# An mLSTM cell whose k-v product is taken as three fp32r products, from parts of v and k that GpSimd splits

## The chip, the cores and the metric

The kernel runs on one NeuronCore of a Trainium2 chip. The metric is the device time of one execution in microseconds (us); the figure compared is the median over runs. Each profile shown is of one execution, whose own time stands beside its span.

## What is computed

The reference is one inference step of a two-layer streaming encoder, for a prompt of 512 tokens and a sample of 64. Layer 1 holds an mLSTM with 4 heads of width 512. The change touches only the state update of the prompt in that cell. Cut to that, the reference reads:

```
dlog = b[t] - b[s] + i[s], masked causal;  m_t = max(inter, max dlog);  w = exp(dlog - m_t)
num  = s_inter * (q C) + ((q k^T) * w) v          # numerator of h
den  = s_inter * (q n) + sum((q k^T) * w)
h    = num / max(|den|, exp(-m_t))
kw   = k * w_s                                     # k weighted by its row of the last token
C_new = dec * C + kw^T v                           # the k-v product: 512 x 512 out of 512 tokens
```

The prompt starts from C = 0, so for it C_new is the product kw^T v alone, written out as the state of 512 x 512 of each head. All of it is in float32.

## The kernel before

Everything stays in one program with one instruction stream for each engine, synchronised by semaphores. Weights come as 1 MB slabs: SyncE loads a slab into `raw` (two buffers), GpSimd splits it into an fp32r high part `whi` and a low part `wlo` (`split`, lines 494 and 501: four pieces of 512 columns, for each a tensor_scalar for the high part and a tensor_tensor subtraction for the low one), and TensorE takes every projection as three fp32r products: high by high, low by high, high by low (`project`, line 596). `split` of slab n waits for `slab_begun` to reach n, that is, for TensorE to have begun slab n-1.

PSUM is used in groups of four banks, alternately even and odd (`group_open`, `group_close`, `group_ready`): a group can be opened only when the group two before it in the order of `schedule()` has been freed by whoever evacuated it.

The mLSTM cell handles the heads in the order 3, 2, 1, 0; the text calls them turn 0, 1, 2 and 3 (n in the code). In each turn TensorE runs, in this order, the groups `smp` (the sample's small products and transposes), `kT` (transposes of k), `den`, `num` (numerator; stationary is v in token order, `mvt`), `kv` (the k-v product), `kvs` (the sample's), `mean`, then the next head's `score`, `var`, and the next head's `vT` (transposes of v). All of these in float32 through the helper `mm` (line 630). `kv` is 16 products a head: for each of 4 output banks d and 4 token blocks j, stationary `mkt[:, j, 128 d ..]`, moving `mvt[:, j, :]` of 512 columns. In turn 2 the four slabs of `ml_out` for the first pair of heads are put in front of `num`, `kv`, `kvs` and `mean`.

Around it:

- VectorE, in turn n from 1 on: `cell_out(n-1)` (lines 2584, 2585 and 2593: twelve instructions that make the output of the head before), then four instructions of line 2625 (k by its weights, for the sum n), which ScalarE adds up (lines 1679, 1680); then the causal mask of the next head (2552), the reciprocal, the scaling of `sz`, the evacuation of `num`, three sums, the evacuation of `kvs` (2659), the subtraction of the mean (2666).
- ScalarE: the copies of v into `mvt` (1578, `turned`), the two high parts of `high_y` (1646), the copies of k into `mkt` (1666), the sums, the issue of the loads of the next head's q, k and v (1685 to 1687), and only then the absolute values of `den` (1690 to 1692), which free the `den` group. `kv` uses the same half of PSUM as `den` and so waits for that.
- GpSimd has no work of the cell's: it has split the slab `ml_out, 1, 0` and waits for turn 2.

```
                act.wait_ge(S("cell_qs"), n + 1)
                load(mq[:], A["t_q"][nxt], "cell_q")
                load(mk[:], A["t_k"][nxt], "cell_k")
                load(mv[:], A["t_v"][nxt], "cell_v")
            g = GR["cell", h, "den"]
            group_ready(act, g)
            act.activation(tm[:, 1, 0:TP], bank(g, 0), ACT.Abs)
```

Of the kernel before, what the change touches and what calls it, by code (L numbers as in the profile page):

```python
# [18 lines left out]
F32 = mybir.dt.float32  # L19
F32R = mybir.dt.float32r  # L20
ALU = mybir.AluOpType
# [3 lines left out]
P = 128  # L25
# [3 lines left out]
T = TP + TS  # L29
HALF = T // 2  # L30
NTB = TP // P
# [4 lines left out]
ML_H, ML_T = 4, 4  # L36
ML_DH = ML_T * P
LATE_Z = (3, "z", 1)
CELL_ORDER = (3, 2, 1, 0)
ATT_ORDER = (0, 2, 1)  # L40
OUT_BEFORE = ("num", "kv", "kvs", "mean")
CELL_STEPS = ("smp", "kT", "den", "num", "kv", "kvs", "mean")
MEM = 256
XH = 4
# [36 lines left out]
MEM_SLABS = [(l, *m) for l in range(2) for m in MEM_ORDER]  # L81
# [111 lines left out]
X_LOADED = (16, 32, 32, 32, 32, 32, 32, 32)  # L193
# [35 lines left out]
def program(nc, A):  # L229
    ctx = ExitStack()  # L230
    with ctx:
        def sb(name, shape, dt=F32, on=ctx):
            return on.enter_context(nc.sbuf_tensor(name, shape, dt))
# [3 lines left out]
        def S(name):  # L237
            if name not in sems:
                sems[name] = ctx.enter_context(nc.semaphore(name))
            return sems[name]  # L240
# [3 lines left out]
        x = xt[:, 0:DT * T].rearrange("p (a t) -> p a t", a=DT)  # L244
        x_in = xt[:, 0:DT * (T + 1)].rearrange("p (a t) -> p a t", a=DT)
        xnh = sb("xnh", [P, DT, T], F32R)
        xnl = sb("xnl", [P, DT, T], F32R)
# [24 lines left out]
        def group_ready(eng, g, turn=None):  # L272
            v = g // 2 + 1
            eng.wait_ge(done[g % 2], v if turn is None else turn + v)
# [108 lines left out]
        cst = sb("conv_out", [P, 2, 16, 3], on=ml)  # L383
        mq = sb("mq", [P, ML_T, T], on=ml)
        mk = sb("mk", [P, ML_T, T], on=ml)
        mv = sb("mv", [P, ML_T, T], on=ml)
        xc = sb("xc", [P, ML_T, T], on=ml)
        mla = ExitStack()
# [6 lines left out]
        gcol = gw[:, 0:48 * 32].rearrange("p (n c) -> p n c", c=32)  # L395
        mla.close()
        mlb = ExitStack()
        rrow = sb("rrow", [4, SCW + TS], on=mlb)
        acol = sb("acol", [P, 20], on=mlb)
        causal = sb("causal", [P, P], on=mlb)  # L400
# [6 lines left out]
        mvt = sb("mvt", [P, NTB, ML_DH], on=mlb)  # L407
# [10 lines left out]
        mlr.close()  # L418
        wt = sb("wt", [P, SCW], on=mlb)
        wts = sb("wts", [TS, TS], on=mlb)  # L420
        mkt = sb("mkt", [P, NTB, ML_DH], on=mlb)
        vt5 = sb("vt5", [TS, ML_DH], on=mlb)
        kt5 = sb("kt5", [TS, ML_DH], on=mlb)
        C0 = sb("C0", [P, ML_T, ML_DH], on=mlb)
        qs = sb("qs", [P, ML_T, TS], on=mlb)
        mlb.close()
        ml.close()

        GR, SL = GROUPS, SLABS
# [51 lines left out]
        def _(pool):  # L481
# [44 lines left out]
            mem0 = SL[("mem",) + MEM_SLABS[0]]  # L526
# [5 lines left out]
            c = slice(0, SLAB // 4)  # L532
# [4 lines left out]
            for kk in range(DT):  # L537
                c = slice(SLAB // 8 * kk, SLAB // 8 * (kk + 1))
# [11 lines left out]
                split(j, mem0 // 2, freed_by=GR["rs", "g", j], parts=2)  # L550
            for j in range(2, len(MEM_SLABS) + 2):
                split(j % 2, mem0 // 2 + j // 2, high=False, act_high=4 * (j - 1) + 3, parts=2)
            third = SL["ml_out", 0, 2]
            with pool.Fori(mem0 // 2 + len(MEM_SLABS) // 2 + 1, third // 2) as i:
                split(0, i)
                split(1, i)
            for j in range(2):
                if j == third % 2:
                    split_by_half(j, third // 2)
                else:  # L560
                    split(j, third // 2)
# [12 lines left out]
        def _(pe):  # L574
# [54 lines left out]
            def mm(out, lhsT, rhs, first=True, last=True):  # L629
                return pe.matmul(out, lhsT, rhs, start=first, stop=last)  # L630
# [60 lines left out]
            for part in ("u", "q", "k", "v", "g"):  # L691
                for i in range(2):
                    g, n = GR["rs", part, i], SL["rs", part, i]
# [392 lines left out]
            for n, h in enumerate(CELL_ORDER):  # L1086
                def open_(x):
                    if h == 1 and x in OUT_BEFORE:
                        out_slab(1, OUT_BEFORE.index(x))
                    g = GR["cell", h, x]  # L1090
                    group_open(pe, g)
                    return g, [bank(g, b) for b in range(4)]

                g, B = open_("smp")
                for d in range(ML_T):
                    mm(B[0][0:TS, 0:TS], mk[:, d, TP:T], mq[:, d, TP:T], d == 0, d == ML_T - 1)
                for b, src in ((1, mv), (2, mk)):
                    for d in range(ML_T):
                        ins = pe.transpose(B[b][0:TS, P * d:P * d + P], src[:, d, TP:T], ident[:])
                group_close(ins, g)  # L1100
                g, B = open_("kT")
                for j in range(NTB):
                    for d in range(ML_T):
                        ins = pe.transpose(B[j][:, P * d:P * d + P], mk[:, d, P * j:P * j + P], ident[:])  # L1104
                group_close(ins, g)
                g, B = open_("den")
                pe.wait_ge(S("cell_pt"), n + 1)
                pe.wait_ge(S("cell_qs"), n + 1)
                pe.wait_ge(S("cell_smp"), n + 1)
                pe.wait_ge(S("cell_c"), 16 * (n + 1))  # L1110
                for d in range(ML_T):
                    mm(B[2][0:TS, :], qs[:, d, :], C0[:, d, :], d == 0, False)
                mm(B[2][0:TS, :], wts[:], vt5[:], False, True).then_inc(S("bank_filled"), 1)
                for j in range(NTB):
                    mm(B[0][:, P * j:TP], ones[:], wt[:, blk(j):blk(j) + TP - P * j], j == 0, j == NTB - 1)
                for d in range(ML_T):
                    mm(B[1][:, 0:TS], n0b[:, d, :], qs[:, d, :], d == 0, False)
                mm(B[1][:, 0:TS], ones[0:TS, :], wts[:], False, True)
                pe.wait_ge(S("bank_read"), n + 1)
                for e in range(ML_T):  # L1120
                    ins = pe.transpose(B[3][:, TS * e:TS * e + TS], tm[0:TS, 1, P * e:P * e + P], ident[0:TS, 0:TS])
                group_close(ins, g)
                g, B = open_("num")
                pe.wait_ge(S("cell_vt"), n + 1)
                for e in range(ML_T):
                    for j in range(NTB):
                        ins = mm(B[e][:, P * j:TP], mvt[:, j, P * e:P * e + P], wt[:, blk(j):blk(j) + TP - P * j],
                                 j == 0, j == NTB - 1)
                group_close(ins, g)
                pe.wait_ge(S("cell_kt"), n + 1)  # L1130
                g, B = open_("kv")
                for d in range(ML_T):
                    for j in range(NTB):
                        ins = mm(B[d], mkt[:, j, P * d:P * d + P], mvt[:, j, :], j == 0, j == NTB - 1)
                        if n + 1 == ML_H and (d, j) == (0, 0):
                            ins.then_inc(S("slab_begun"), 1)
                group_close(ins, g)
                g, B = open_("kvs")
                for d in range(ML_T):
                    ins = mm(B[d], kt5[:, P * d:P * d + P], vt5[:])  # L1140
                    if d + 1 < ML_T:
                        ins.then_inc(S("kvs_part"), 1)
                group_close(ins, g)
                if h == 1:
                    out_slab(1, 3)
                pe.wait_ge(S("cell_sum"), 2 * n + 1)
                token_sum(GR["cell", h, "mean"], 1, ss)
                if n + 1 < ML_H:
                    cell_scores(n + 1)
                else:  # L1150
                    out_slab(0, 0, order=(4, 5, 6, 7), stop=False, close=False, first=False, half=True)
                pe.wait_ge(S("cell_sum"), 2 * n + 2)
                if n + 1 < ML_H:
                    token_sum(GR["cell", h, "var"], 1, ss)
                    cell_values(n + 1)
# [17 lines left out]
        def _(act):  # L1173
            ch = Chain(act, S("act_step"))

            def load(dst, src, sem):
                act.dma_start(dst, src).then_inc(S(sem), 16)
# [256 lines left out]
                gelu(h)  # L1434
                memory_out(MEM_SLABS[4 * h + 3], high=h != 1)
            act.wait_ge(S("fin_copied"), RET_H)
            load(x, A["xT"][:, :, 0:T], "x_again")
            for a in range(2):
                g = GR["glu", a]
                group_ready(act, g)  # L1440
# [216 lines left out]
            for n, h in enumerate(CELL_ORDER):  # L1657
# [24 lines left out]
                if nxt is not None:  # L1682
                    factors_in(n + 1)
                    act.wait_ge(S("cell_qs"), n + 1)
                    load(mq[:], A["t_q"][nxt], "cell_q")
                    load(mk[:], A["t_k"][nxt], "cell_k")
                    load(mv[:], A["t_v"][nxt], "cell_v")
                g = GR["cell", h, "den"]
                group_ready(act, g)
                act.activation(tm[:, 1, 0:TP], bank(g, 0), ACT.Abs)  # L1690
# [2 lines left out]
                        free[g % 2], S("cell_abs"))  # L1693
                g = GR["cell", h, "kv"]
                group_ready(act, g)
                for d in range(ML_T):
                    ins = act.activation(mvt[:, d, :], bank(g, d), ACT.Copy)
                ch.mark(ins, free[g % 2])
# [51 lines left out]
        def _(v):  # L1750
# [346 lines left out]
            for h in range(RET_H):  # L2097
# [24 lines left out]
                for j in range(NTB):  # L2122
                    at = TP - 1 - P * j
# [79 lines left out]
                add_squares(i, (6, 7))  # L2203

            v.sem_inc(S("arena_free"), 1)
            v.wait_ge(S("x_again"), 16)
            residual_and_norm([GR["rs_out", i] for i in range(4)], 1, "cross0")

            def attention(l):
# [635 lines left out]
```

## Time and profile before

| | |
|---|---|
| time, median of 3 runs | 2202.43 us (2201.35 to 2204.22) |
| the profiled execution's own time | 2201.16 us |
| its span, first to last instruction | 2199.4 us |
| TensorE busy | 2156.8 us (98%) |
| VectorE, ScalarE, GpSimd busy | 1244.7, 423.2, 1203.1 us |
| granted TensorE clock, mean | 0.998 |

Busy time is the sum of an engine's instructions, an idle time stands before the instruction that ended it, and "<-" names what released it. The cell's four turns lie between 1317 and 1604 us of the span.

### The profile page before, as it was taken

To read this page: it belongs to the slowest core of one execution; us is meant where nothing else is said; L and a number is where in the kernel's file an instruction comes from. 1 tells how busy PE (TensorE), PEld (TensorE's weight loads), DVE (VectorE), ACT (ScalarE), POOL (GpSimd) and SP (SyncE) were. 2 spreads that over 40 slices of the span, in tenths; PEclk is the share of its full clock that TensorE was granted. 3 is DMA by queue.
4 is the path that set the end of the run, shared out by engine and by line. 5 is a ranking of instruction groups with operands and counts; after the bars stand their busy time and mean duration, and the time that the engine had idled before them with its cause. 6 is when DMAs were issued, how large, how long until landed. Compare 5 with 4: busy or idle time off the path is not lost. (4 is left out here: it accounts for less than half of the span.)

```text
span 2199.4 us, 38981 instructions
## 1 busy us (share of the span) xinstructions
PE 2156.8 (98%) x15839; PEld 2019.4 (92%) x15839; DVE 1244.7 (57%) x2095; ACT 423.2 (19%) x780; POOL 1203.1 (55%) x1228
## 2 busy tenths in 40 slices
PE   9989899999999999999999999999999999999998
PEld 9988789989999999999999995587699999999997
DVE  6888875454625344676557645772754364435263
ACT  6224541222000000121202113421422220000002
POOL 7675666526656655666657650032254365665663
PEclk9999999999999999999999999999999999999999
DMA  6224344212222222224433323552332122222221
GB/s 219 77 87 145 112 144 192 78 39 78 77 95 78 77 82 89 76 92 153 152 145 136 142 100 141 203 192 78 120 137 75 39 79 95 77 79 94 77 78 62
DMA packets 41809, 235.95 MB, mean 107 GB/s; under 512 B 4672, under 2 KB 10048, under 8 KB 16584
## 3 DMA queue, kind: packets, MB, share of 16 engines
q1 hardware_dynamic: 24512, 157.57, 20.2%
q10 hardware_dynamic: 17160, 76.38, 9.1%
q8 instruction: 106, 1.74, 0.3%
q14 instruction: 31, 0.25, 0.0%
HBM read 200.05 MB, written 33.89 MB: 106 GB/s over the span
## 5 line engine op out<-in xcount | busy, mean ns | idle before, releaser
L501 POOL TENSOR_TENSOR wlo<-raw,whi 128x512 fp32r<-128x512 f32 (+1 forms) x684 | 827.4, 1219 | 112.6 <-ACT whi L1253 69.9
L494 POOL TENSOR_SCALAR whi<-raw 128x512 fp32r<-128x512 f32 x512 | 365.3, 714 | 824.1 <-PE psum L596 771.3
L596 PE MATMUL psum<-xnh,whi 128*128 128x288 f32 (+1 forms) x2784 | 607.6, 296 | 13.2 <-DVEq L210 3.6
L596 PE MATMUL psum<-xnh,wlo 128*128 128x288 f32 (+1 forms) x2784 | 603.9, 295 | 0.0
L596 PE MATMUL psum<-xnl,whi 128*128 128x288 f32 (+1 forms) x2784 | 603.8, 295 | 0.0
L596 PEld LDWEIGHTS psum<-xnh,whi 128*128 128x128 f32 x2784 | 451.9, 189 | 20.4 <-issue 11.8
L596 PEld LDWEIGHTS psum<-xnh,wlo 128*128 128x128 f32 x2784 | 451.8, 189 | 0.0
L596 PEld LDWEIGHTS psum<-xnl,whi 128*128 128x128 f32 x2784 | 451.8, 189 | 0.0
L596 PE MATMUL psum<-hh,whi 128*128 128x288 f32 x992 | 212.0, 295 | 2.1 <-DVE hl L2330 2.1
L596 PE MATMUL psum<-hl,whi 128*128 128x288 f32 x992 | 211.8, 294 | 0.0
L596 PE MATMUL psum<-hh,wlo 128*128 128x288 f32 x992 | 210.7, 293 | 0.0
L2338 DVE TENSOR_TENSOR x<-x,psum 128x288 f32<-128x288 f32 x124 | 48.0, 450 | 257.5 <-PE psum L596 257.5
L596 PEld LDWEIGHTS psum<-hh,whi 128*128 128x128 f32 x992 | 158.0, 187 | 4.0 <-DVE hl L2330 4.0
L596 PEld LDWEIGHTS psum<-hh,wlo 128*128 128x128 f32 x992 | 158.6, 188 | 0.0
L596 PEld LDWEIGHTS psum<-hl,whi 128*128 128x128 f32 x992 | 158.3, 188 | 0.0
L2319 DVE SCALAR_TENSOR_TENSOR hr<-psum,rs 128x288 f32<-128x288 f32 x128 | 49.7, 451 | 153.2 <-PE psum L596 138.1
L1210 ACT ACTIVATE tm<-x 128x576 f32<-128x576 f32 x54 | 35.2, 679 | 521.2 <-DVEq L2342 378.4
L2187 DVE TENSOR_TENSOR x<-x,psum 128x288 f32<-128x288 f32 x80 | 30.9, 447 | 141.9 <-PE psum L596 141.9
L2326 DVE CAST hh<-hs 128x288 fp32r<-128x288 f32 x128 | 107.5, 899 | 4.7
L1223 ACT ACTIVATE xnh<-x,par 128x576 fp32r<-128x576 f32 x40 | 28.8, 769 | 413.6 <-DVEq L2342 388.4
L2330 DVE TENSOR_TENSOR hl<-hs,hh 128x288 fp32r<-128x288 f32 x128 | 91.5, 773 | 1.1
L2422 DVE SCALAR_TENSOR_TENSOR xc<-xm,par,xc 128x512 f32<-128x512 f32 x96 | 87.1, 947 | 1.7
(459 smaller groups left out, 2766.1 us busy)
## 6 DMA issues: line engine op xcount, KB each, us to landing
raw<-in_w SPq DMA_DIRECT2D x145, 1024.0 KB, 4.8
C<-in_C ACTq DMA_DIRECT2D x4, 1024.0 KB, 4.8
o_cp<-mvt ACTq DMA_DIRECT2D x4, 1024.0 KB, 3.9
o_cs<-C ACTq DMA_DIRECT2D x4, 1024.0 KB, 6.5
t_xc<-xc ACTq DMA_DIRECT2D x3, 1152.0 KB, 7.3
t_z<-mv ACTq DMA_DIRECT2D x3, 1152.0 KB, 4.1
t_q<-mq ACTq DMA_DIRECT2D x3, 1152.0 KB, 4.2
t_k<-mk ACTq DMA_DIRECT2D x3, 1152.0 KB, 4.2
```

The costliest lines, as they stand in the source:

```text
L494: pool.tensor_scalar(whi[:, s, c], raw[:, s, c], 1.0, 1.0, ALU.mult, ALU.mult).then_inc(S("slab_hi"), 1)
L501: ins = pool.tensor_tensor(wlo[:, s, c], raw[:, s, c], whi[:, s, c].bitcast(F32), ALU.subtract)
L596: ins = pe.matmul(bank(g, 2 * m + b)[:, 0:t1 - t0], W[wi][:, kk, m0 + m, :], r[:, kk, t0:t1], start=(at_first and wi == 0 and r is rh), st ...
L1210: act.activation(tm[:, kk % 2, :], x[:, kk, :] if i else x_in[:, kk, 0:T], ACT.Square).then_inc(S("sq_ready"), 1)
L1223: ins = act.activation(xnh[:, kk, :], x[:, kk, :], ACT.Copy, scale=col(gain, kk))
L2187: ins = tt(halves(x, 2 * i + m)[b], halves(x, 2 * i + m)[b], bank(g, 2 * m + b)[:, 0:HALF], ADD)
L2319: ch.mark(stt(hr[:, b, :], B[b], 0.0, RS[b % 2], ALU.max, MUL))
L2326: ch.mark(v.tensor_copy(halves(hh, 2 * i + b // 2)[b % 2], hs[:, b, :]))
L2330: ins = tt(halves(hl, 2 * i + b // 2)[b % 2], hs[:, b, :], h_.bitcast(F32), SUB)
L2338: ins = tt(xx, xx, bank(g, 2 * m + b)[:, 0:HALF], ADD)
L2422: ins = stt(dst, src, wc, dst, MUL, ADD)
```

## The change

1. `cell_split(n)` is new on GpSimd. For the first m token blocks of head n (m = 4, 4, 2, 4 in turns 0 to 3) it makes a high and a low part of v (m tensor_scalar, then m tensor_tensor) as soon as `mvt` stands, and of k in pairs of blocks as soon as `mkt` stands. Turns 0 to 2 are done behind the split of slab `ml_out, 1, 0`, turn 3 behind that of `ml_out, 0, 0`. The `Fori` over the slabs around it is written out.
2. `kv` on TensorE runs over j outside and d inside. A block j < m takes three fp32r products of 512 columns for each d, and waits for its own parts; the two other blocks of turn 2 stay one float32 product for each d.
3. The high part of k lies where `mv` lies, the low part of k on top of `mkt`; the parts of v lie in free rows of `xnh` and `xnl`, in turn 2 in two new tiles.
4. Since k's high part lies on `mv`, the load of the next head's v moves on ScalarE's queue from behind those of q and k to behind the end of `kv`.
5. The semaphore `x_again` is merged into another one, in layer 0; the same transfer, the same wait.

```
+CELL_SPLIT = (4, 4, 2, 4)
...
+            def cell_split(n):
+                m, at = CELL_SPLIT[n], 4 * CELL_SPLIT_BY[n]
+                pool.wait_ge(S("cell_vt"), n + 1)
+                for j in range(m):
+                    pool.tensor_scalar(mv_split(n, j)[0], mvt[:, j, :], 1.0, 1.0, ALU.mult, ALU.mult).then_inc(S("cell_split"), 1)
+                for j in range(m):
+                    pool.wait_ge(S("cell_split"), at + m + j)
+                    hi, lo = mv_split(n, j)
+                    pool.tensor_tensor(lo, mvt[:, j, :], hi.bitcast(F32), ALU.subtract).then_inc(S("cell_split"), 1)
+                at += 2 * m
+                pool.wait_ge(S("cell_kt"), n + 1)
+                for j0 in range(0, m, 2):
+                    for j in (j0, j0 + 1):
+                        pool.tensor_scalar(mkh[:, j, 0:ML_DH], mkt[:, j, :], 1.0, 1.0, ALU.mult, ALU.mult).then_inc(S("cell_split"), 1)
+                    for j in (j0, j0 + 1):
+                        pool.wait_ge(S("cell_split"), at + 2 * j0 + 2 + (j - j0))
+                        pool.tensor_tensor(mkl[:, j, :], mkt[:, j, :], mkh[:, j, 0:ML_DH].bitcast(F32), ALU.subtract).then_inc(S("cell_split"), 1)
...
+            for n in range(first // 2 * 2, third // 2 * 2):
+                split(n % 2, n // 2)
+                if n == first:
+                    for head in range(3):
+                        cell_split(head)
+                if n == SL["ml_out", 0, 0]:
+                    cell_split(3)
...
-                for d in range(ML_T):
-                    for j in range(NTB):
-                        ins = mm(B[d], mkt[:, j, P * d:P * d + P], mvt[:, j, :], j == 0, j == NTB - 1)
...
+                for j in range(NTB):
+                    if j < m:
+                        pe.wait_ge(S("cell_split"), at + 2 * (j - j % 2) + 3 + j % 2)
+                    for d in range(ML_T):
+                        c = slice(P * d, P * d + P)
+                        if j < m:
+                            hi, lo = mv_split(n, j)
+                            ins = mm(B[d], mkh[:, j, c], hi, j == 0, False)
...
+                            mm(B[d], mkl[:, j, c], hi, False, False)
+                            ins = mm(B[d], mkh[:, j, c], lo, False, j == NTB - 1)
+                        else:
+                            ins = mm(B[d], mkt[:, j, c], mvt[:, j, :], False, j == NTB - 1)
...
-                    load(mv[:], A["t_v"][nxt], "cell_v")
                 g = GR["cell", h, "den"]
...
                 g = GR["cell", h, "kv"]
                 group_ready(act, g)
+                if nxt is not None:
+                    load(mv[:], A["t_v"][nxt], "cell_v")
```

## Rows read from the trace of the kernel before

**Rows 1.** Busy time of the engines, and the granted clock in 40 slices.
```profile
PE 2156.8 (98%) x15839; PEld 2019.4 (92%) x15839; DVE 1244.7 (57%) x2095; ACT 423.2 (19%) x780; POOL 1203.1 (55%) x1228
...
PEclk9999999999999999999999999999999999999999
```

**Rows 2.** Timeline of TensorE, turns 0, 1, 2 and 3 (start, length, instruction).
```profile
1354.23 13.90 PE L630 MATMUL psum<-mvt,mkt 128*128 128x512 f32 x32
...
1406.28 13.97 PE L630 MATMUL psum<-mvt,mkt 128*128 128x512 f32 x32 [0.33 <-ACTq L210]
...
1470.60 0.51 PE L596 MATMUL psum<-xnh,whi 128*128 128x288 f32 x2
...
1587.23 1.24 PE L630 MATMUL psum<-ss,over 128*128 128x288 f32 x4 [0.55 <-DVEq L2678]
```

**Rows 3.** Timeline of TensorE in layer 1's attention, first and last of ten fp32r products.
```profile
1711.66 0.39 PE L630 MATMUL psum<-pTh,Vl 128*128 128x512 f32 x1
...
1713.70 0.39 PE L630 MATMUL psum<-pTh,Vl 128*128 128x512 f32 x1
```

**Rows 4.** Timeline of GpSimd: last piece before the cell, first pieces in it.
```profile
1310.79 0.62 POOL L494 TENSOR_SCALAR whi<-raw 128x512 fp32r<-128x512 f32 x1
1311.49 1.29 POOL L501 TENSOR_TENSOR wlo<-raw,whi 128x512 fp32r<-128x512 f32 x1
1449.88 1.03 POOL L494 TENSOR_SCALAR whi<-raw 128x512 fp32r<-128x512 f32 x1 [137.11 <-PE psum L596]
1450.99 1.67 POOL L501 TENSOR_TENSOR wlo<-raw,whi 128x512 fp32r<-128x512 f32 x1
1452.63 1.12 POOL L494 TENSOR_SCALAR whi<-raw 128x512 fp32r<-128x512 f32 x1
1453.84 1.68 POOL L501 TENSOR_TENSOR wlo<-raw,whi 128x512 fp32r<-128x512 f32 x1
```

**Rows 5.** Timeline of VectorE in turn 1, GpSimd idle.
```profile
1388.82 0.82 DVE L2584 SCALAR_TENSOR_TENSOR tm<-sz,par,rs 128x576 f32<-128x576 f32 x1 [0.68 <-DVE kt L2616]
...
1398.81 0.76 DVE L2593 TENSOR_TENSOR xnl<-ss,xnh 128x576 fp32r<-128x576 f32 x1
...
1402.43 0.76 DVE L2625 SCALAR_TENSOR_TENSOR tm<-mk,factors_all 128x576 f32<-128x576 f32 x1
...
1421.34 3.32 DVE L2659 SCALAR_TENSOR_TENSOR C<-C,factors_all,psum 128x512 f32<-128x512 f32 x4 [2.62 <-PE psum L630]
```

**Rows 6.** Timeline of VectorE in turn 2, GpSimd at work on a slab until 1460.5.
```profile
1450.58 0.94 DVE L2593 TENSOR_TENSOR xnl<-ss,xnh 128x576 fp32r<-128x576 f32 x1
1451.74 1.53 DVE L2625 SCALAR_TENSOR_TENSOR ss<-mk,factors_all 128x576 f32<-128x576 f32 x1 [0.23 <-DVE xnl L2593]
1453.20 1.16 DVE L2625 SCALAR_TENSOR_TENSOR tm<-mk,factors_all 128x576 f32<-128x576 f32 x1
1454.31 1.83 DVE L2625 SCALAR_TENSOR_TENSOR ss<-mk,factors_all 128x576 f32<-128x576 f32 x1
...
1468.58 1.54 DVE L2187 TENSOR_TENSOR x<-x,psum 128x288 f32<-128x288 f32 x4
```

**Rows 7.** Timeline of ScalarE in turns 0 and 1 (ACTq is a transfer issued).
```profile
1368.17 2.06 ACT L1697 ACTIVATE mvt<-psum 128x512 f32<-128x512 f32 x4 [20.24 <-PE psum L630]
...
1392.99 2.40 ACT L1666 ACTIVATE mkt<-psum,wcol 128x512 f32<-128x512 f32 x4
...
1404.58 0.47 ACTq L1177 DMA_DIRECT2D mv<-t_v  x1
1405.10 0.60 ACT L1690 ACTIVATE tm<-psum 128x512 f32<-128x512 f32 x1 [0.91 <-issue]
...
1405.70 0.39 ACT L1692 ACTIVATE qs<-psum 128x256 f32<-128x256 f32 x1
```

**Rows 8.** Timeline of VectorE in turn 3.
```profile
1576.58 3.32 DVE L2659 SCALAR_TENSOR_TENSOR C<-C,factors_all,psum 128x512 f32<-128x512 f32 x4 [1.39 <-PE psum L630]
```

**Rows 9.** Transfers issued from 1340 to 1392 us (median us from issue to landing).
```profile
mv<-t_v ACTq DMA_DIRECT2D x1, 1152.0 KB, 12.6
```

More of the change, by code:

```diff
@@ L41 @@
 OUT_BEFORE = ("num", "kv", "kvs", "mean")
+CELL_SPLIT = (4, 4, 2, 4)
+CELL_SPLIT_BY = [sum(CELL_SPLIT[:n]) for n in range(ML_H + 1)]
 CELL_STEPS = ("smp", "kT", "den", "num", "kv", "kvs", "mean")
@@ L385, in program @@
         mk = sb("mk", [P, ML_T, T], on=ml)
+        mvs = ExitStack()
+        mkh = sb("mkt_high", [P, ML_T, T], F32R, on=mvs)
+        mvs.close()
         mv = sb("mv", [P, ML_T, T], on=ml)
@@ L397, in program @@
         mlb = ExitStack()
+        rrs = ExitStack()
+        mvh2 = sb("mvt_high", [P, 2, ML_DH], F32R, on=rrs)
+        rrs.close()
         rrow = sb("rrow", [4, SCW + TS], on=mlb)
@@ L420, in program @@
         wts = sb("wts", [TS, TS], on=mlb)
+        mks = ExitStack()
+        mkl = sb("mkt_low", [P, NTB, ML_DH], F32R, on=mks)
+        mks.close()
         mkt = sb("mkt", [P, NTB, ML_DH], on=mlb)
@@ L425, in program, with mv_split @@
         qs = sb("qs", [P, ML_T, TS], on=mlb)
+        mvl2 = sb("mvt_low", [P, 2, ML_DH], F32R, on=mlb)
+        def mv_split(n, j):
+            if CELL_SPLIT[n] < NTB:
+                return mvh2[:, j, :], mvl2[:, j, :]
+            return xnh[:, j, 0:ML_DH], xnl[:, j, 0:ML_DH]
         mlb.close()
@@ L552, in _ @@
                 split(j % 2, mem0 // 2 + j // 2, high=False, act_high=4 * (j - 1) + 3, parts=2)
-            third = SL["ml_out", 0, 2]
-            with pool.Fori(mem0 // 2 + len(MEM_SLABS) // 2 + 1, third // 2) as i:
+            def cell_split(n):
[15 more added lines that the diff above has]
+                        pool.tensor_tensor(mkl[:, j, :], mkt[:, j, :], mkh[:, j, 0:ML_DH].bitcast(F32), ALU.subtract).then_inc(S("cell_split"), 1)
+            third, first = SL["ml_out", 0, 2], SL["ml_out", 1, 0]
+            with pool.Fori(mem0 // 2 + len(MEM_SLABS) // 2 + 1, first // 2) as i:
                 split(0, i)
                 split(1, i)
+            for n in range(first // 2 * 2, third // 2 * 2):
[5 more added lines that the diff above has]
+                    cell_split(3)
             for j in range(2):
@@ L1131, in _ @@
                 g, B = open_("kv")
-                for d in range(ML_T):
-                    for j in range(NTB):
-                        ins = mm(B[d], mkt[:, j, P * d:P * d + P], mvt[:, j, :], j == 0, j == NTB - 1)
-                        if n + 1 == ML_H and (d, j) == (0, 0):
-                            ins.then_inc(S("slab_begun"), 1)
+                m, at = CELL_SPLIT[n], 4 * CELL_SPLIT_BY[n] + 2 * CELL_SPLIT[n]
+                for j in range(NTB):
[6 more added lines that the diff above has]
+                            ins = mm(B[d], mkh[:, j, c], hi, j == 0, False)
+                            if n + 1 == ML_H and (d, j) == (0, 0):
+                                ins.then_inc(S("slab_begun"), 1)
+                            mm(B[d], mkl[:, j, c], hi, False, False)
+                            ins = mm(B[d], mkh[:, j, c], lo, False, j == NTB - 1)
+                        else:
+                            ins = mm(B[d], mkt[:, j, c], mvt[:, j, :], False, j == NTB - 1)
                 group_close(ins, g)
@@ L1436, in _ @@
             act.wait_ge(S("fin_copied"), RET_H)
-            load(x, A["xT"][:, :, 0:T], "x_again")
+            load(x, A["xT"][:, :, 0:T], "x_loaded0")
             for a in range(2):
@@ L2205, in _ @@
             v.sem_inc(S("arena_free"), 1)
-            v.wait_ge(S("x_again"), 16)
+            v.wait_ge(S("x_loaded0"), X_LOADED[0] + 16)
             residual_and_norm([GR["rs_out", i] for i in range(4)], 1, "cross0")
```

## The prediction

> **What bounds the kernel now.** I read the busy times first: TensorE is busy 98% of the span, every other engine 57% or less, and the granted clock is at its full level, 2.4 GHz, in all 40 slices [rows 1]. So a microsecond taken off TensorE's stream is gained, as long as TensorE then doesn't wait for somebody. Then TensorE's timeline through the cell, for who that somebody would be. The k-v product takes 13.9 us a head [rows 2]. In turn 1 TensorE has waited 0.33 us for ScalarE just before it, and at 1587.23, in turn 3, 0.55 us for VectorE [rows 2]: small waits, but they say that ScalarE and VectorE arrive there no earlier than TensorE does. The timelines of VectorE, ScalarE and GpSimd show why, and they are what this forecast turns on. GpSimd is idle for 137 us from slab `ml_out, 1, 0` until turn 2 [rows 4]. It looks free, but VectorE isn't indifferent to it.
>
> **Step 1, the product itself.** A float32 product of 512 columns costs 13.90 / 16 = 0.869 us (a record pair is one product) [rows 2]. An fp32r product of the same 128x128 by 512, with its weights changed each time as in the new `kv`, stands in the attention: from the first to the last of ten rows nine steps take 2.04 us, 0.227 us each [rows 3]. Three are 0.68. So a head with m = 4 takes 48 x 0.227 = 10.9 us, a gain of 3.0; turn 2 with m = 2 takes 24 x 0.227 + 8 x 0.869 = 12.4, a gain of 1.5. Together 3 x 3.0 + 1.5 = 10.5 us. The bounds of this term are narrow, 0.2 us a head.
>
> **Step 2, GpSimd's new work.** A head with m = 4 adds 8 tensor_scalar and 8 tensor_tensor. With nobody in the way a pair costs 0.62 + 1.29 and small gaps, 1.96 us, so 7.9 us for v and 7.9 us for k [rows 4]. v can be split from the moment `mvt` stands (in turn 1 about 1386.7), k from the end of the `mkt` copies, 1395.4 [rows 7], and TensorE begins `kv` at 1406.3 [rows 2] and needs block j only 2.7 us after block j-1. So GpSimd is in time for `kv`: this step alone costs nothing, even if each piece is slowed as below. It is hidden by the kT, den and num groups; without these it would be the whole 15.8 us.
>
> **Step 3, what it does to VectorE.** This is the term of most weight. In turn 2 of the kernel before, GpSimd's slab split falls on the instructions of line 2625. Those take 0.76 us when GpSimd is idle [rows 5] and 1.53, 1.16 and 1.83 when it works [rows 6]. GpSimd suffers too: its tensor_scalar starts come 1.64 us after the tensor_tensor in front, and the tensor_tensor 1.21 us after the tensor_scalar, where 0.62 + 1.29 were enough [rows 4]. The two take turns, instruction by instruction, when VectorE reads two tensors from SBUF. The instructions of `cell_out` (lines 2584, 2585, 2593) are of that kind, and in turns 1 and 3 they run today with GpSimd idle: twelve, from 1388.82, with steps of (1398.81 - 1388.82) / 11 = 0.91 us [rows 5].
>
> Turn 1 in the new kernel: three of v's tensor_scalar fit in before 1388.8. The fourth and the four tensor_tensor meet `cell_out`, and all 8 instructions of k meet the rest of it and line 2625, which are 16 instructions of VectorE in all, up to 1403.2 [rows 5]. That makes 13 meetings, 5 with a tensor_scalar at 1.21 - 0.91 = 0.30 us, 8 with a tensor_tensor at 1.64 - 0.91 = 0.73 us: 7.4 us by which line 2625 ends later. From below, the least touched row is 0.94 instead of 0.76 [rows 6], 13 x 0.18 = 2.3 us; from above, the longest is 1.83 instead of 0.76, 13.9 us. I take 7.4, since it is made from GpSimd's own steps in a stretch of the same kind.
>
> The Trainium skill (SBUF — State Buffer, "Who interferes with whom") says that a VectorE instruction with two SBUF inputs and a GpSimd instruction that reads SBUF exclude each other for the whole instruction. The trace agrees with the fact and not with the size: a full exclusion would give steps of 0.82 + 0.62 and 0.82 + 1.29, and they are 1.21 and 1.64 [rows 4, 5]. Taken literally it is a rival below.
>
> **Step 4, who waits for VectorE.** Behind line 2625 stand ScalarE's sums, then its loads, then the absolute values of `den`, which free the half of PSUM that `kv` opens; they end at 1405.70 + 0.39, and `kv` begins at 1406.28 after waiting for them [rows 2, 7]. So in turn 1 the delay of VectorE goes to TensorE whole, less 0.5 us for the issue of v's load, which no longer stands in front [rows 7]: 6.9 us. The earlier hold-ups on the same way (k's copies come later too, and `num` needs them) lie inside it. Turn 1: +6.9 - 3.0 = +3.9.
>
> Turn 0 has no `cell_out`; the few instructions that meet k's split there cost about 1 us, `kv` starts 6 us after its PSUM is free, VectorE idles long before the `kvs` evacuation. It keeps its gain: -3.0.
>
> Turn 2 splits half as much. New meetings are two tensor_tensor of v and four instructions of k, since the slab's own split meets VectorE already: 4 x 0.73 + 2 x 0.30 = 3.5 us. Slab `ml_out, 1, 1` starts at 1470.60 and needs the evacuation of `ml_out, 1, 0`, which VectorE ends at 1468.58 + 1.54 = 1470.12 [rows 2, 6]: slack 0.5, stall 3.0, +1.5 after the gain. The slab's own split begins some 5 us later and has 10 us to spare.
>
> Turn 3 is like turn 1, 7.4 us on VectorE. There VectorE also bounds the end: it evacuates `kvs` after only 1.39 us of idle time [rows 8] and TensorE waits for its sum of squares at 1587.23 [rows 2]. A shorter `kv` takes nothing off that but these 1.39 us. So +6.0, with the gain of `kv` already in it.
>
> **Step 5, the load of v.** It is issued at the end of `kv`, about 1365 in turn 0, and used by the transposes at about 1379. Today it lands in 12.6 us behind the two other 1152 KB loads [rows 9]; now it has the queue nearly to itself, and even 12.6 fits. It puts one issue of 0.47 us before the copies of `kv` [rows 7]; `mean` has more than 1 us in hand there. Its traffic shares the queues with the store of C; that store is not used for 14 us. Price nothing, at worst 1 us a turn in two turns. The merged semaphore and the unrolled slab loop: nothing.
>
> **Sum.** -3.0 + 3.9 + 1.5 + 6.0 = +8.4 us on the profiled execution's 2201.2 us (span 2199.4 and 1.8 around it), which gives 2209.6. The median of the runs is 1.3 us above that execution, so I say 2210.5. The rest of the kernel after 1604 us is bound by TensorE and moves rigidly. With d for the delay of VectorE in a full turn, the sum is about 2.5 d - 10: it is zero at d = 4.0 us.
>
> **Rivals.**
>
> A. The change gains. GpSimd's instructions slip into the gaps of `cell_out` (its steps of 0.91 hold instructions of 0.76 to 0.82), and d stays at or below 2.3. For it: the least touched row [rows 6], and GpSimd's lead in v's split. Against it: rows of 1.53 and 1.83 in the same stretch. With d = 0 the gains are 3.0, 3.3 (the wait of 0.33 goes too), 1.5 and, in turn 3, only 1.5: -9.3, 2193; at d = 2.3 it is -4.2, 2198. This decides as long as d is below 4.0.
>
> B. About the same, d between 3.5 and 5: half the meetings, because VectorE waits for ScalarE's high parts now and then and GpSimd gets by. -1.3 to +2.5, 2201 to 2205.
>
> C. Full exclusion: 5 x (1.44 - 0.91) + 8 x (2.11 - 0.91) = 12.3 us; 2.5 x 12.3 - 10 = +21, 2223. Against it: the steps measured in rows 4 and the fact that VectorE has only 16 such instructions to be held. The page for it is the one named in step 3.
>
> D. The k parts are late for `kv`, so that TensorE waits for GpSimd itself. In turn 1 k's second pair would end near 1409.6, and `kv` would have to begin at 1406.3 and reach block 2 at 1411.7. It costs at most 1 to 2 us and only where VectorE's delay is small; it lowers A's gain, 2195.
>
> **How the numbers follow.** About 0.2% is what a measurement of this kernel can tell from no change, 4.4 us: faster is below 2198, slower above 2206.8. The forecast (d from 5.5 to 9, so 2206 to 2215) has a chance of 0.60, C 0.05, B 0.14, A with D 0.21. Slower is the forecast and C, 0.65; same is B with the edge of A, 0.16; faster 0.19. The range reaches from 2195.5, in A, to 2217; about 0.12 is left out below and 0.06 above. The likeliest case's own range is 2205 to 2216.
>
> **What would show it.** Right: `kv` of 10.9 us or less in its own steps; lines 2584, 2585 and 2625 in turns 1 and 3 at 1.2 to 1.8 us instead of 0.76 to 0.82; a wait of about 7 us on ScalarE in front of `kv` in turn 1 and 6 in turn 3 (there or before the last sums), 3 us on VectorE before slab `ml_out, 1, 1`; GpSimd's idle time cut. Wrong: those lines unchanged, or lengthened with no wait on TensorE; or `kv` waiting for GpSimd, which is D; or a wait of the transposes of v for their load, which would make step 5 the culprit.

## The result, and the profile after

The changed kernel is slower: 2216.62 us median of 4 runs (2213.39 to 2216.99), beside 2201.89 us for the kernel before (4 runs, 2199.63 to 2204.22, the three shown above among them). The ratio is 1.006, with a 95% interval from 1.0048 to 1.0072, which is 13.2 us by the ratio and 14.7 by the medians. The forecast had 8.1 by the medians (2210.5 against 2202.43). The profiled execution took 2213.39 us, 12.2 more than that of the kernel before (2201.16), where the sum of the steps said 8.4.

The page of the changed kernel, to be held against [rows 1]:

```profile
PE 2156.6 (98%) x15895; PEld 2035.2 (92%) x15895; DVE 1265.5 (57%) x2095; ACT 423.5 (19%) x780; POOL 1267.1 (57%) x1284
...
PEclk9999999999999999999999999999999999999999
```

GpSimd has 64.0 us more work in 56 more instructions, and VectorE has 20.8 us more in the same 2095 instructions: the same work, slower. TensorE is busy for as long as before, though the product became shorter. The table below follows TensorE from turn to turn (profiled executions, us from the span's start):

| milestone | before | after | shift |
|---|---|---|---|
| turn 0: `kv` begins | 1354.23 | 1354.32 | +0.1 |
| turn 0: `kvs` begins | 1368.06 | 1365.59 | -2.5 |
| turn 1: `kv` begins | 1406.28 | 1410.55 | +4.3 |
| turn 1: `kvs` begins | 1420.18 | 1423.38 | +3.2 |
| turn 2: VectorE evacuates `ml_out, 1, 0` | 1468.58 | 1475.29 | +6.7 |
| turn 2: `mean` begins | 1526.59 | 1531.71 | +5.1 |
| turn 3: VectorE evacuates `kvs` | 1576.58 | 1587.65 | +11.1 |
| turn 3: the last sums | 1587.23 | 1598.24 | +11.0 |

So turn 0 gives -2.5, turn 1 +5.7, turn 2 +1.9 and turn 3 +5.9. TensorE's timeline of the changed kernel, turns 0, 1, 2 and 3, answers to [rows 2]:

```profile
1354.32 0.48 PE L673 MATMUL psum<-xnh,mkt_high 128*128 128x512 f32 x1
...
1365.59 3.70 PE L673 MATMUL psum<-vt,kt 64*128 64x512 f32 x8
...
1396.44 0.46 PE L1164 MATMUL psum<-ident,tm 64*128 64x64 f32 x4 [1.26 <-ACT tm L1722]
1396.83 10.59 PE L673 MATMUL psum<-wt,mvt 128*128 128x512 f32 x32
1410.55 0.77 PE L673 MATMUL psum<-xnh,mkt_high 128*128 128x512 f32 x1 [3.13 <-issue]
1411.11 0.63 PE L673 MATMUL psum<-xnh,mkt_low 128*128 128x512 f32 x1
1411.54 0.63 PE L673 MATMUL psum<-xnl,mkt_high 128*128 128x512 f32 x1
...
1415.66 0.39 PE L673 MATMUL psum<-xnh,mkt_high 128*128 128x512 f32 x1
1415.89 0.39 PE L673 MATMUL psum<-xnh,mkt_low 128*128 128x512 f32 x1
...
1477.03 0.51 PE L639 MATMUL psum<-xnh,whi 128*128 128x288 f32 x2 [1.81 <-DVEq L2244]
...
1598.24 1.24 PE L673 MATMUL psum<-ss,over 128*128 128x288 f32 x4 [0.55 <-DVEq L2732]
```

In turn 0 the 48 products take 1365.59 - 1354.32 = 11.27 us, 0.235 each. In turn 1 there are two waits, for ScalarE before the transposes of line 1164 and before `kv` ("issue" stands where no semaphore event is left to name; below it is followed to ScalarE), and behind each wait the same products run slower: at 1411 a product begins every 0.43 us, at 1415.7 every 0.23, and `num` takes 10.59 us where 8.90 is its usual time. The windows of turn 1 show why (columns: busy time of each engine, then the granted clock, DMA share and GB/s):

```profile
1390.00:1396.00 6.00, 5.18 (x22) 2.81 (x20) 5.63 (x5) 3.20 (x6) 3.68 (x4) 1.00 0.00 0
1396.00:1398.00 2.00, 1.56 (x6) 0.98 (x7) 1.71 (x3) 0.96 (x2) 1.92 (x3) 0.72 0.00 0
1398.00:1400.00 2.00, 2.00 (x5) 0.88 (x4) 1.93 (x2) 0.00 (x0) 1.92 (x2) 0.50 0.00 0
1400.00:1402.00 2.00, 2.00 (x9) 1.31 (x8) 1.74 (x2) 0.68 (x1) 2.00 (x2) 0.93 0.00 0
...
1410.00:1412.00 2.00, 1.45 (x4) 1.19 (x5) 1.41 (x2) 0.40 (x3) 0.00 (x0) 0.63 0.86 326
1412.00:1414.00 2.00, 2.00 (x6) 1.61 (x5) 2.00 (x1) 0.00 (x0) 0.00 (x0) 0.51 0.99 406
1414.00:1424.00 10.00, 10.00 (x43) 7.71 (x43) 8.75 (x10) 0.14 (x1) 0.00 (x0) 1.00 0.37 151
```

The granted clock stands at 0.50, its lower level of 1.2 GHz, for a part of each of the two stretches. The page's row in tenths hides this; one slice is 55 us long, and a 9 only says 90% or more. For the same reason the prediction read too much in [rows 1] when it took the clock as full in all 40 slices: in the kernel before it stands at 0.50 from 2192 us to the end. I had not foreseen the drops in the cell.

VectorE's timeline in turn 1, against [rows 5]:

```profile
1387.31 1.71 DVE L2639 SCALAR_TENSOR_TENSOR tm<-xc,par,tm 128x576 f32<-128x576 f32 x1
1389.16 1.60 DVE L2638 SCALAR_TENSOR_TENSOR ss<-sz,par,rs 128x576 f32<-128x576 f32 x1
1390.80 1.71 DVE L2639 SCALAR_TENSOR_TENSOR ss<-xc,par,ss 128x576 f32<-128x576 f32 x1
1392.65 1.60 DVE L2647 TENSOR_TENSOR xnl<-tm,xnh 128x576 fp32r<-128x576 f32 x1
1394.40 0.82 DVE L2638 SCALAR_TENSOR_TENSOR tm<-sz,par,rs 128x576 f32<-128x576 f32 x1
1395.25 0.82 DVE L2639 SCALAR_TENSOR_TENSOR tm<-xc,par,tm 128x576 f32<-128x576 f32 x1
1396.22 0.93 DVE L2647 TENSOR_TENSOR xnl<-ss,xnh 128x576 fp32r<-128x576 f32 x1
...
1403.80 1.82 DVE L2679 SCALAR_TENSOR_TENSOR tm<-mk,factors_all 128x576 f32<-128x576 f32 x1
...
1407.29 0.74 DVE L2679 SCALAR_TENSOR_TENSOR tm<-mk,factors_all 128x576 f32<-128x576 f32 x1
```

GpSimd's timeline at the same time, and in turn 0 for comparison:

```profile
1325.61 5.31 POOL L579 TENSOR_TENSOR xnl<-mvt,xnh 128x512 fp32r<-128x512 f32 x4
...
1384.31 2.36 POOL L575 TENSOR_SCALAR xnh<-mvt 128x512 fp32r<-128x512 f32 x4 [37.24 <-ACTq L212]
1386.76 6.88 POOL L579 TENSOR_TENSOR xnl<-mvt,xnh 128x512 fp32r<-128x512 f32 x4
1395.80 1.83 POOL L584 TENSOR_SCALAR mkt_high<-mkt 128x512 fp32r<-128x512 f32 x2 [2.16 <-ACTq L212]
...
1403.36 3.39 POOL L587 TENSOR_TENSOR mkt_low<-mkt,mkt_high 128x512 fp32r<-128x512 f32 x2
```

While GpSimd subtracts, each of these two-input instructions of VectorE takes 1.6 to 1.8 us; beside a tensor_scalar of GpSimd (1396.22) it takes 0.93; in GpSimd's pause from 1393.6 to 1395.8 they are back at 0.82. GpSimd pays too: four subtractions take 6.88 us here and 5.31 in turn 0. Line 2679 ends at 1408.03, where before it ended at 1403.18: 4.85 later, and 7.3 later once the 2.5 that turn 0 had gained are counted. ScalarE's timeline, against [rows 7], has the link to TensorE:

```profile
1408.88 0.24 ACT L1733 ACTIVATE tm<-tm 128x64 f32<-128x64 f32 x1
...
1409.42 0.60 ACT L1742 ACTIVATE tm<-psum 128x512 f32<-128x512 f32 x1 [0.21 <-issue]
...
1410.01 0.39 ACT L1744 ACTIVATE qs<-psum 128x256 f32<-128x256 f32 x1
```

The last sum over line 2679's output is added up, then come the absolute values that free PSUM, up to 1410.40, and `kv` begins at 1410.55. TensorE's waits from 1310 to 1630 us (us in total, times, longest) put the sizes together:

```profile
PE psum L673 <- issue: 5.9, 2, 3.1
PE psum L1164 <- ACT tm L1722: 4.0, 3, 2.1
...
PE psum L639 <- DVEq L2244: 1.8, 1, 1.8
```

For turn 3 the row of VectorE that answers to [rows 8] has its idle time gone:

```profile
1587.65 3.27 DVE L2713 SCALAR_TENSOR_TENSOR C<-C,factors_all,psum 128x512 f32<-128x512 f32 x4 [0.16 <-PE psum L673]
```

### The profile page after: what moved, and what is told of

Read it like the earlier page. It is cut to its first block, busy times and chain, and to the rows that moved or that the text cites. A ratio compares the mean times of both kernels' runs of the same rounds, so it can differ in the third digit from the quotient of the medians.

```text
span 2211.6 us, 39108 instructions
## 1 busy us (share of the span) xinstructions
PE 2156.6 (98%) x15895; PEld 2035.2 (92%) x15895; DVE 1265.5 (57%) x2095; ACT 423.5 (19%) x780; POOL 1267.1 (57%) x1284
## 4 chain that ended last, share of the span: by engine, by line
PE 83%; DVE 11%; ACT 2%; issue 2%; POOL 1%; DMA 1%; ACTq 0%; DVEq 0%; POOLq 0%
PE psum L639 67%; PE psum L673 11%; PE psum L659 3%; DVE hl L2384 1%; DVE hh L2380 1%; DVE xc L2476 1%; PE psum L689 1%; DVE xnl L2075 1%; ACT whi L1306 0%; DVE hr L2373 0%; DVE hs L2376 0%; POOL wlo L518 0%; PE psum L1015 0%; DVE tm L2639 0%; PE psum L669 0%
```

## The experiments

Two sets of kernels, each set on one chip with the kernel before beside it: the first four against 2204.51 us (16 runs), the other four against 2203.85 (33 runs). The changed kernel itself was not run in either set, so it is compared with them through the kernel before. The theory is that of the prediction: the product gains what its steps say, and GpSimd's reads hold up VectorE, which passes it on through ScalarE's chain. The rivals: GpSimd's work costs by itself or by its writes; the moved load is to blame.

The traces give a second measure beside the times: how much more or less a kernel takes than the kernel before from the start of `kv` in turn 0 to the last sums of turn 3 (1354.23 to 1587.23 there). It leaves out what lies outside that stretch, where each of the nine traces below is 1 to 7 us longer than that of the kernel before.

| kernel | whole time, by the ratio | that stretch, by the trace |
|---|---|---|
| changed kernel | +13.2 | +10.9 |
| splits alone | +22 | +20.4 |
| product alone | -7.9 | -9.3 |
| load alone | -0.9 | -0.6 |
| writes without reads | -7.3 | -8.9 |
| turn 0 alone | -3.1 | -2.0 |
| half in the later turns | +2.6 | +3.7 |
| another place | -4.2 | -4.7 |
| the same, and turn 3 | -6.4 | -6.1 |

**Splits alone.** The product stays float32, GpSimd makes all parts; those of k are written over those of v, behind one more wait between the two. v is loaded late.

```
-                            hi, lo = mv_split(n, j)
-                            ins = mm(B[d], mkh[:, j, c], hi, j == 0, False)
+                            ins = mm(B[d], mkt[:, j, c], mvt[:, j, :], j == 0, j == NTB - 1)
...
```

> The changed kernel with its splits on GpSimd, its waits, its loop order and its late load of v, but with the k-v product in float32 as before; the parts of k go to the rows of the parts of v and nobody reads any part. Theory 1 (GpSimd's reads hold up VectorE, and through ScalarE's den copies TensorE): all of the loss and none of the gain. From the changed kernel's own trace 6.7 us in turn 1, 3.3 in turn 2, 6.9 in turn 3, and 2 to 4 for the lower clock that follows the waits: 17 to 21 us slower than the kernel before, about 2221. Theory 2 (the late load of v, or its traffic): the same as e3_load, whatever that is. Theory 3 (TensorE waits for the parts themselves): within 2 us of the kernel before, since a product of 13.9 us needs each block later.

Measured: 2225.41 us (4 runs), ratio 1.0100 (1.0083 to 1.0117), about 21 slower. The waits of TensorE in the cell are the same as in the changed kernel: 6.0 us at `kv`, 4.5 before line 1165, 1.8 behind `ml_out, 1, 0`. So the splits alone bring the whole loss.

**Product alone.** The three fp32r products of a tile, all from the same two tiles, which are written rounded; GpSimd does nothing. The product is thus summed three times into the state, and the split is left out.

```
-                            hi, lo = mv_split(n, j)
-                            ins = mm(B[d], mkh[:, j, c], hi, j == 0, False)
+                            k_, v_ = mkt[:, j, c], mvt[:, j, :]
+                            ins = mm(B[d], k_, v_, j == 0, False)
```

> Three fp32r products a tile as in the changed kernel, but GpSimd does nothing in the cell: the copies of v and k are written as fp32r and all three products read these same two tiles, so the low parts are left out (the states of the prompt and the numerator are those of rounded k and v). Loop order and late load of v as in the changed kernel. Theory 1: the whole gain, 2.5 us in turn 0, 3 in turn 1, 1.5 in turn 2 and only about 1.5 in turn 3, where VectorE bounds the end: 8 to 9 us faster than before, about 2193. Theory 2: less than that by what e3_load loses. Theory 3: as theory 1.

Measured: 2195.22 us (5 runs), ratio 0.9964 (0.9949 to 0.9978), 7.9 us faster by the interval's middle. With the 22 us that the splits alone cost by their ratio that makes +14, and the change cost 13.2 by its ratio and 14.7 by the medians: the two parts add up, within intervals of 3 to 4 us either way on each.

**Load alone.** v loaded behind `kv`, blocks outside and d inside, float32 product, no split.

```
-                if n == first:
-                    for head in range(3):
-                        cell_split(head)
```

> The late load of v and the new loop order alone: float32 product, no splits. Theory 1: no change, within 1 us of the kernel before (2201 to 2203). Theory 2: this carries the loss, 10 us or more slower.

Measured: 2202.91 us (10 runs), ratio 0.9996 (0.9987 to 1.0006). No price can be seen, and by the interval it is at most 1.3 us; the load as the culprit is out.

**Writes without reads.** As the product alone, and GpSimd writes zeros to the rows of the parts, at the same places and behind the same waits, with two fills for each subtraction. It reads nothing.

```
-                    pool.tensor_tensor(lo, mvt[:, j, :], hi.bitcast(F32), ALU.subtract).then_inc(S("cell_split"), 1)
+                    pool.memset(lo.bitcast(F32), 0.0)
+                    pool.memset(hi.bitcast(F32), 0.0).then_inc(S("cell_split"), 1)
```

> As e2_products, but GpSimd is busy in the cell at the same places and with the same waits as in the changed kernel: instead of each split instruction it fills a tile with zeros (one fill of 512 columns for a tensor_scalar, two for a tensor_tensor), so it writes to SBUF and reads nothing. TensorE waits for it as in the changed kernel. Theory 1, by way of the reads: VectorE keeps its 0.76 to 0.82 us, and the time is that of e2_products within 1 us, about 2193. If GpSimd's being busy, its queue or its writes are the cause: 8 to 20 us slower than e2_products.

Measured: 2196.24 us (6 runs), ratio 0.9967 (0.9954 to 0.9979), the same as with GpSimd idle. VectorE's timeline of this kernel in turn 1:

```profile
1388.49 0.82 DVE L2642 SCALAR_TENSOR_TENSOR tm<-xc,par,tm 128x576 f32<-128x576 f32 x1
1389.46 0.82 DVE L2641 SCALAR_TENSOR_TENSOR ss<-sz,par,rs 128x576 f32<-128x576 f32 x1
1390.31 0.82 DVE L2642 SCALAR_TENSOR_TENSOR ss<-xc,par,ss 128x576 f32<-128x576 f32 x1
```

and GpSimd's:

```profile
1388.61 0.53 POOL L579 MEMSET xnl<- 128x512 f32 x1
1389.08 0.53 POOL L580 MEMSET xnh<- 128x512 f32 x1
1389.66 0.53 POOL L579 MEMSET xnl<- 128x512 f32 x1
1390.13 0.53 POOL L580 MEMSET xnh<- 128x512 f32 x1
```

GpSimd is busy without a gap and VectorE keeps its 0.82 us. So it isn't that GpSimd works, waits and signals there, nor that it writes: what VectorE loses to are instructions of GpSimd that read SBUF. A fill is shorter than a subtraction (0.53 against 1.29 us, 12 fills for v's 8 instructions), so the cover is not as long as in the changed kernel, but where both run nothing is lost.

**Turn 0 alone.** `CELL_SPLIT = (4, 0, 0, 0)`; the other turns keep the float32 product.

> CELL_SPLIT = (4, 0, 0, 0): the split and the fp32r products in turn 0 alone, where no cell_out runs on VectorE. Theory 1: the gain of one product without a loss, 2.5 us faster than before (turn 0 of the changed kernel gained 2.5), 2200 beside 2202.5. A rival by which each split costs TensorE something of its own would give no gain.

Measured: 2200.41 us (11 runs), ratio 0.9986 (0.9975 to 0.9996), 3.1 us faster. Turn 0 has no `cell_out`, and keeps its gain: its `kv` takes 11.27 us again (1358.47 to 1369.74).

**Half in the later turns.** `CELL_SPLIT = (4, 2, 2, 2)`.

> CELL_SPLIT = (4, 2, 2, 2): half the splits in turns 1 and 3. Theory 1 with one meeting at a time: in turns 1 and 3 VectorE is held up by two tensor_tensor of v (two tensor_scalar fit in before) and four instructions of k, 4 x 0.73 + 2 x 0.30 = 3.5 us; turn 1: 3.5 - 0.8 - 1.5 = +1.2, turn 3: 3.5 - 1.4 = +2.1, turn 2 as in the changed kernel +1.9, turn 0 -2.5: 2.7 us slower than before, 1 to 6, and 12 faster than the changed kernel, since without the long waits the clock stays up. If the loss were one of the waits for the parts or of the fp32r products, halving would save half of it at most.

Measured: 2205.27 us (10 runs), ratio 1.0012 (1.0002 to 1.0022), 2.6 us slower. TensorE's wait before `kv` in turn 1 is now 2.15 us, and that of line 1164 in the whole cell 1.0 us; `num` takes its 8.90. The clock did not stay up, as the expectation had it: behind that wait it stands at 0.50 between 1412 and 1414 us, and `kv` of turn 1 takes 14.17 us, while in turn 3, behind 0.53 and 1.69 us of waits, it stays at 1.00 and `kv` takes 12.59. The price goes down with the number of meetings. The traced execution took 2211.34 us, 6 more than the median; its `kv` of turn 0 begins 4.0 us later than in the kernel before, so its traces are read inside the cell only.

**Another place.** Turn 0 as in the change. In turn 1 only the last two blocks, split from the absolute values of `den` on, when VectorE has `cell_out` and line 2679 behind it; in turn 2 the last two, behind the splits of the slabs `ml_out, 1, 1` and `1, 2`; in turn 3 none.

```
-CELL_SPLIT = (4, 4, 2, 4)
+CELL_SPLIT = (4, 2, 2, 0)
...
+                pool.wait_ge(S("cell_abs"), n + 1)
+                for j in range(NTB - m, NTB):
...
+                if n == SL["ml_out", 1, 2]:
+                    cell_split(2)
```

> Splits put where VectorE has room: turn 0 all four blocks early; turn 1 only the last two blocks, from the moment den is freed (TensorE takes the two other blocks first, as float32); turn 2 the last two blocks, behind the split of slab ml_out 1, 2, where VectorE is idle; turn 3 none. Theory 1: -2.5, -1.3, -1.4 and 0: 5 us faster than before, about 2197.5 beside 2202.5, and faster than e5_turn0 by 2.7. If GpSimd's splits cost TensorE something wherever they stand: no faster than e5_turn0.

Measured: 2199.87 us (11 runs), ratio 0.9981 (0.9971 to 0.9991), 4.2 us faster. Against turn 0 alone, which was to be beaten by 2.7 us, that is 1.1 by the ratios, and the two intervals overlap: the times don't show that the splits in turns 1 and 2 gained. The traces do, -4.7 against -2.0 us in the cell, with `kv` of turn 1 at 12.52 us and no wait in front of it.

**The same, and turn 3's last two blocks from the same point**, `CELL_SPLIT = (4, 2, 2, 2)`.

> As e7_late, with the last two blocks of turn 3 too, from the moment den is freed. There VectorE bounds the end and GpSimd's split of the next slab follows at once. Theory 1: 0 to 3 us slower than e7_late, since the gain of 1.5 is not on the path and the meetings are. If TensorE bounds turn 3: 1.5 us faster than e7_late.

Measured: 2198.01 us (10 runs), ratio 0.9971 (0.9962 to 0.9981), 6.4 us faster: clearly ahead of the kernel before. That it is also ahead of the version without turn 3's parts can't be told from the times, since the intervals overlap; the traces say so, and by them the expectation was wrong: turn 3 gained. From the start of `num` to the last sums it takes 33.11 us here (1549.72 to 1582.83) and 34.38 without turn 3's parts (1552.14 to 1586.52). VectorE's timeline of turn 3, without them:

```profile
1564.45 2.60 DVE L2715 TENSOR_TENSOR sz<-sz,tm 128x2304 f32<-128x2304 f32 x1
1567.08 1.38 DVE L2716 TENSOR_TENSOR sz<-sz,qs 128x256 f32<-128x256 f32 x1
...
1571.00 1.85 DVE L2725 TENSOR_TENSOR ss<-sz 128x576 f32<-128x576 f32 x1
...
1575.87 3.32 DVE L2738 SCALAR_TENSOR_TENSOR C<-C,factors_all,psum 128x512 f32<-128x512 f32 x4 [1.43 <-PE psum L693]
```

and with them:

```profile
1562.13 2.69 DVE L2715 TENSOR_TENSOR sz<-sz,tm 128x2304 f32<-128x2304 f32 x1
1564.86 0.72 DVE L2716 TENSOR_TENSOR sz<-sz,qs 128x256 f32<-128x256 f32 x1
...
1568.11 1.06 DVE L2725 TENSOR_TENSOR ss<-sz 128x576 f32<-128x576 f32 x1
1569.20 1.74 DVE L2726 TENSOR_TENSOR ss<-ss,sz 128x576 f32<-128x576 f32 x1
1570.98 1.05 DVE L2727 TENSOR_TENSOR ss<-ss,sz 128x576 f32<-128x576 f32 x1
...
1572.18 3.31 DVE L2738 SCALAR_TENSOR_TENSOR C<-C,factors_all,psum 128x512 f32<-128x512 f32 x4 [0.16 <-PE psum L693]
```

VectorE's idle time before the evacuation of `kvs` falls from 1.43 to 0.16 us, and that is the gain. What VectorE lost in all did not become more. The split of the slab met it there already: 1.38 and 1.85 us where turn 1, without it, has 0.42 and 0.76 (lines 2637 and 2646 of the kernel before), 2.0 us together. With the new parts, which took its place while it moved behind, lines 2715 to 2727 are lengthened by 0.1, 0.3, 0.3, 1.0 and 0.3, again 2.0. The large instruction of line 2715 cost GpSimd something and VectorE almost nothing here: GpSimd's tensor_scalar at 1562.38 took 2.92 us in its shadow, and line 2715 took 2.69 us instead of 2.60. That isn't always so: in the product alone it began at 1558.65, during a subtraction of GpSimd's slab split, and took 3.34 us.

## Why the prediction was right in direction and short in size

The measured 2216.62 us lie above the forecast's 2206 to 2215, 0.6 above the likeliest case's own 2205 to 2216, and just inside the whole range, which ends at 2217. The direction and the path came as forecast, and three of the four turns within 0.5 us; the loss was 13 to 15 us instead of 8.

**Step 1, the product.** The mechanism was right, the term a little large: 11.27 us a head at the full clock and not 10.9, 0.235 us for a product and not 0.227, 2.5 us gained in turn 0 and not 3.0. What it gained in all, with GpSimd idle, is 7.9 us by the times, where 10.5 was the term. In the trace of the product alone the cell gains 9.3 us, and turn 3 gives 2.5 of them, not the 1.5 that the prediction allowed it with GpSimd idle: VectorE's idle time before the evacuation of `kvs` falls from 1.39 to 0.16 us, it loses 1.5 us to the slab's split instead of 2.0, and from the evacuation to the subtraction behind it 2.97 us pass instead of 3.74. The profiled executions differ by 6.5 us only; most of the missing 2.8 stands behind the cell and is told under the sum.

**Step 2, GpSimd's own work.** Right. k's last part of turn 1 is done at 1406.75, `kv` begins at 1410.55, and TensorE waits for no part; rival D did not happen.

**Step 3, the delay of VectorE.** Right in mechanism, and near the number: 7.3 us in turn 1 where 7.4 was forecast from GpSimd's steps in [rows 4]. The 13 meetings came, 8 with a subtraction and 5 with a tensor_scalar. That the total fits so well is partly luck: the 8 cost 6.65 us by VectorE's steps, where 5.8 was forecast, and the 5 cost 0.7, where 1.5 was. Writes alone lengthen no instruction of VectorE, so reads it is. The Trainium skill (SBUF — State Buffer, "Who interferes with whom") puts the conflict at a port that VectorE's second operand shares with GpSimd; that only reading instructions of GpSimd cost agrees with it, the fills beside 0.82 us instructions being the number. Its full exclusion, rival C, does not hold: 12.3 us of delay were asked for, 7.3 came.

**Step 4, who waits.** Turn 1's stall before the clock is looked at: 1410.55 - 1406.28 + 2.5 = 6.8 us, forecast 6.9. It doesn't all stand in front of `kv`, as the prediction's signs had it: 3.13 us do, where 0.33 did before, 1.26 before line 1164, 0.84 at 1387.01 for the load of `in_C`, and 1.69 is `num` at the lower clock. Turn 2: VectorE 3.5 us late at `ml_out, 1, 0` (6.7 less the 3.2 it came in with), forecast 3.5; the turn +1.9, forecast +1.5. Turn 3: +5.9, forecast +6.0. What failed is turn 1's net, +3.9 forecast and +5.7 measured. Of these 1.8 us, 1.56 are a term that stood nowhere in the sum: TensorE, after its waits, gets the lower clock, and `kv` takes 1423.38 - 1410.55 = 12.83 us instead of 11.27. `num` pays 1.69 in the same way (10.59 against 8.90), but that lies inside the wait for ScalarE behind it. Turn 3 has the same drop and the same 12.83 us; there VectorE bounds the end, and the drop costs at most the 0.16 us for which VectorE still waits. That the drop comes with the waits is read over the traces and not from an experiment made for it. Those of the changed kernel, the splits alone and half the blocks, all with a wait of 2.15 us or more before `kv` in turn 1, show 0.50 to 0.51 in a window soon behind it, and `kv` of the splits alone takes 15.6 us (1415.06 to 1430.66) instead of 13.9. Those of the kernel before, turn 0 alone and the writes, with no such wait there, show 1.00 through it, and so do the four others. But a wait does not decide it alone. At 131 us, far ahead of the cell, TensorE waits 2.3 us for GpSimd in all ten traces; seven then show the lower clock (turn 0 alone 0.50 between 132 and 134 us), and three do not, the kernel before and the changed kernel among them. In turn 0 of the cell four of the ten traces (the writes, turn 0 alone, half, another place) show 0.50 or 0.51 about 1330 us, behind a wait of 0.76 to 0.79 us; the kernel before has a wait of 0.76 there, and 1.00. So a wait is a chance of the drop and not a fixed price, and how often the changed kernel pays the 1.56 us is not known.

**Step 5, the load.** Right: no price alone, no wait of the transposes of v, and the load lands in 5.1 us at the end of turn 0, where it took 12.6 [rows 9].

**The sum.** With -2.5, +5.7, +1.9 and +5.9 the four turns make +11.0 us where the sum had 8.4: 0.5 is turn 0's product, 1.6 turn 1's clock, the rest small. The profiled executions differ by 12.2, so 1.2 us come after the cell. They stand in four weight slabs of the MLP (the feed-forward part) that follows, where nothing was changed: VectorE's evacuations there come every 12.48 us in the kernel before (1893.58, 1906.07) and every 12.80 in the changed one (1904.87, 1917.67), at a granted clock of 1.00 in both. The kernel before has eight such faster slabs, the changed kernel and the load alone have four, the seven others none. So the product alone gives back 2.5 us there. The cause is open, and so is whether it belongs to the kernel or to the execution; it goes against the prediction's sentence that the rest moves rigidly. And the profiled execution of the changed kernel, with 2213.39 us, is at least 3.1 us faster than each of its other three runs (2216.52 to 2216.99), whose clock means are 0.992 to 0.995 where it has 0.995. These runs have no trace. More of the lower clock would fit them: in the trace of turn 0 alone, drops at about 132, 160, 244 and 1330 us go with a `kv` of turn 0 that begins 4.2 us later than in the kernel before. But the mean of one of the three is no lower, so what those 3 us are stays open.

## What to carry to other kernels

An idle engine isn't free for work that reads SBUF: look at what runs on VectorE at that time, count its two-input SBUF instructions, and follow the chain behind them to whoever frees the PSUM that TensorE waits for. If the work must go there, put it where VectorE has nothing that others wait for, or behind instructions that GpSimd meets anyway; with 4, 2, 2 and 2 blocks a turn the kernel was 2.6 us slower with the splits in one place and 6.4 faster with them in another. And when a sum turns a busy stretch of TensorE into a stretch with a wait, give the slower clock behind the wait a term of its own, with a range from nothing to what it costs: here 1.6 us for a `kv`, in three of three traces with a wait of 2.15 us or more before it in turn 1, but not behind every such wait elsewhere.

## What was not expected of the hardware

Waits of TensorE of 0.72, 0.84 and 1.26 us between 1383 and 1396.4 us, in a stretch where it was otherwise busy, were followed by a granted clock of 0.50, 1.2 GHz, for some 3 to 4 us (0.72, 0.50 and 0.93 in windows of 2 us); one of 3.13 us was followed by the same (0.63, 0.51). Products of 512 columns then begin every 0.43 us instead of every 0.23. A wait of 2.3 us at 131 us was followed by the lower clock in seven of ten traces, and by 1.00 in the three others. At the same granted clock of 1.00, products of 288 columns in the MLP begin every 0.130 us in some slabs and every 0.133 in others, which makes 12.48 or 12.80 us for a slab. GpSimd's fills beside VectorE's two-input instructions cost neither anything (0.53 and 0.82 us), while a subtraction of 1.29 us beside an instruction of 0.82 makes a common step of about 1.7 us (GpSimd's four took 6.88), less than their sum of 2.11, and a tensor_scalar of 0.62 costs such an instruction only 0.1 to 0.2 us.
